# Three of four z blocks turned by VectorE, the second output product over two column blocks at a time, and the identity first on SP's queue

## What is computed

```python
def conformer_mixer(hn, w_in, b_in, w_dw, b_dw, ln_g, ln_b, w_out, b_out):
    proj = hn @ w_in
    ab = proj[..., :2 * CONV_WIDTH] + b_in
    z = proj[..., 2 * CONV_WIDTH:]
    a, g = jnp.split(ab, 2, axis=-1)
    u = a * jax.nn.sigmoid(g)
    u = lax.conv_general_dilated(
        u, w_dw[:, None, :].astype(u.dtype), window_strides=(1,),
        padding=((CONV_K - 1, 0),), dimension_numbers=('NWC', 'WIO', 'NWC'),
        feature_group_count=CONV_WIDTH) + b_dw
    u = jax.nn.silu(layer_norm(u, ln_g, ln_b))
    return (u * jax.nn.silu(z)) @ w_out + b_out
...
        x = x + rms_norm(y, post_norm_g[i])
```

## Time and profile before

| | |
|---|---|
| median of 3 runs | 850.21 us (847.71 to 851.01) |
| the profiled execution | 850.66 us, its span 848.9 us |
| TensorE busy | 837.6 us, 99% of the span |
| VectorE, ScalarE, GpSimd busy | 684.5, 428.2, 336.4 us |
| DMA | 159.49 MB, mean 188 GB/s |

### The profile page before, as it was taken

How to read it: one execution, slowest core, us unless ns; L and a number is a source line. 1 busy time by engine, 2 the same in 40 slices (tenths; PEclk the granted TensorE clock), 3 DMA queues, 4 the chain that set the end, 5 groups by cost and what they waited for, 6 DMA issues and landing times.

```text
span 848.9 us, 12103 instructions
## 1 busy us (share of the span) xinstructions
PE 837.6 (99%) x3873; PEld 695.4 (82%) x3873; DVE 684.5 (81%) x1179; ACT 428.2 (50%) x592; POOL 336.4 (40%) x169
## 2 busy tenths in 40 slices
PE   8999999999999999999999999999999999999996
PEld 6888888888888888888888788888888888888884
DVE  4688799988999799968656629999999999566555
ACT  5744544455444645454445674545444554574441
POOL 0243004500441014400000299888888878772000
PEclk9999999999999999999999999999999999999999
DMA  9956655656467545746655366555655546556522
GB/s 320 293 164 199 195 151 171 194 182 198 150 189 213 188 150 170 225 148 219 215 188 193 129 199 199 187 174 184 198 179 172 194 156 198 191 212 236 197 98 99
DMA packets 97509, 159.49 MB, mean 188 GB/s; under 512 B 3300, under 2 KB 38468, under 8 KB 97092
## 3 DMA queue, kind: packets, MB, share of 16 engines
q1 hardware_dynamic: 97284, 158.97, 58.5%
q10 hardware_dynamic: 192, 0.08, 0.0%
HBM read 156.94 MB, written 2.10 MB: 187 GB/s over the span
## 4 chain that ended last, share of the span: by engine, by line
PE 97%; issue 1%; DMA 1%; DVE 0%; ACT 0%; DVEq 0%; POOLq 0%; POOL 0%; ACTq 0%
PE acc L420 29%; PE acc L422 29%; PE acc L421 29%; PE X L430 2%; PE acc L405 1%; PE acc L407 1%; PE acc L406 1%; PE acc L501 1%; PE acc L486 1%; DMA ident<-in_identity 1%; PE X L560 0%; PE X L545 0%; PE X L544 0%; PE X L561 0%; PE X L559 0%
## 5 line engine op out<-in xcount | busy, mean ns | idle before, releaser
L773 ACT ACTIVATE w_hi<-raw 128x1024 fp32r<-128x1024 f32 x282 | 298.8, 1061 | 354.4 <-PE acc L422 354.0
L420 PE MATMUL acc<-w_hi,xT_hi 128*128 128x512 f32 x864 | 339.0, 392 | 0.1
L422 PE MATMUL acc<-w_hi,xT_lo 128*128 128x512 f32 x864 | 336.5, 389 | 0.0
L421 PE MATMUL acc<-w_lo,xT_hi 128*128 128x512 f32 x864 | 336.2, 389 | 0.0
L1059 DVE TENSOR_TENSOR w_lo<-raw,w_hi 128x1024 fp32r<-128x1024 f32 x182 | 245.7, 1366 | 78.9 <-ACT w_hi L773 76.6
L1518 POOL TENSOR_TENSOR w_lo<-raw,w_hi 128x1024 fp32r<-128x1024 f32 x100 | 243.1, 2438 | 48.9 <-ACT w_hi L773 48.7
L422 PEld LDWEIGHTS acc<-w_hi,xT_lo 128*128 128x128 f32 x864 | 162.2, 188 | 34.0
L420 PEld LDWEIGHTS acc<-w_hi,xT_hi 128*128 128x128 f32 x864 | 162.3, 188 | 33.1 <-DVE xT_lo L1078 0.3
L421 PEld LDWEIGHTS acc<-w_lo,xT_hi 128*128 128x128 f32 x864 | 162.3, 188 | 32.9
L1343 DVE SCALAR_TENSOR_TENSOR X<-u_pad,taps,X 128x256 f32<-128x256 f32 x464 | 182.5, 480 | 0.0
L1481 POOL TENSOR_TENSOR small<-small 128x1 f32<-128x1 f32 (+1 forms) x7 | 4.3, 618 | 232.9 <-DVE small L1289 124.2
(11 more groups left out here) (151 smaller groups left out, 755.0 us busy)
## 6 DMA issues: line engine op xcount, KB each, us to landing
raw<-in_w_in SPq DMA_DIRECT2D x78, 1024.0 KB, 5.3
raw<-in_w_in SPq DMA_DIRECT2D x66, 512.0 KB, 4.4
raw<-in_w_out SPq DMA_DIRECT2D x32, 1024.0 KB, 5.0
gpost<-in_post_g SPq DMA_DIRECT2D x2, 1024.0 KB, 5.0
xrow<-in_x SPq DMA_DIRECT2D x4, 256.0 KB, 5.5
raw<-in_w_in SPq DMA_DIRECT2D x4, 256.0 KB, 4.9
xrow<-in_x SPq DMA_DIRECT2D x2, 512.0 KB, 10.0
bout<-in_b_out SPq DMA_DIRECT2D x1, 1024.0 KB, 7.3
```

What stands on the lines that cost most here:

```text
L420: nc.tensor.matmul(a, hi[:, k, rows], w_hi[:, slot, i], start=(k == 0), stop=False)
L421: nc.tensor.matmul(a, hi[:, k, rows], w_lo[:, slot, i], start=False, stop=False)
L422: last = nc.tensor.matmul(a, lo[:, k, rows], w_hi[:, slot, i], start=False, stop=(k == KT - 1))
L773: nc.scalar.activation(w_hi[:, slot], raw[:, u % LOADS, 2 * half:2 * half + 2], ACT.Copy).then_inc(hi_ready[slot], 1)
```

## The change

- `ident` is loaded first on SP's queue instead of second on ScalarE's. Four of the seven `keep_clock` matmuls stand ahead of the wait, three between the transpose of the norm gains and that of x.
- z blocks 0 to 2 are no longer turned by TensorE. VectorE turns them in SBUF with `turn` (four instructions of 32 x 32 block transposes a step, four steps a block) into a new buffer `zT`, which lies where `c_row` did. `gate` reads blocks 0 to 2 there in one instruction each; block 3 is turned by TensorE as before (`last_gate_T`), now without a wait for gate 2.
- The output product goes through column blocks 0 and 1 together, four k tiles of each in turn (`OUT1_ORDER`), then blocks 2 and 3 as before. The loads, the waits for `vT_lo` (now ahead of slices 0, 4, 8, 12), the reading of blocks 0 and 1 (`OUT1_LAST`, behind the splits of slices 17 and 19) and the sums of squares follow.
- ScalarE rounds the gated blocks behind slices 0, 3, 5 and 9 (`FINAL_AT`) instead of 0, 2, 4 and 6, and writes z rows of block 3 ahead of the second.
- GpSimd splits slices 0 to 9 (`OUT1_POOL`) instead of 0 to 7.
- `gpost1` and `bout` are loaded into the space of `xT_lo`, once the last z slice is multiplied, instead of over `z_row1` once the last z transposes are done.

```diff
-GATE_AT = (26, 28, 30)
+OUT1_ORDER = tuple([(n, k + i) for k in (0, 2, 4, 6) for n in (0, 1) for i in (0, 1)]
+                   + [(n, i) for n in (2, 3) for i in range(SLICES)])
+OUT1_LAST = (13, 15, 23, 31)
+OUT1_POOL = 10
+FINAL_AT = (0, 3, 5, 9)
...
-        gpost1 = at("gpost1", B + 16 * KB, [P, D])
-        bout = at("bout", B + 24 * KB, [P, D])
+        zT = at("zT", B, [P, KT - G, SEQ])
+        gpost1 = at("gpost1", A + 16 * KB, [P, D])
+        bout = at("bout", A + 24 * KB, [P, D])
...
+            sp.dma_start(ident[:], identity).then_inc(ident_in, 16)
             x_load(0, 0)
...
             for j in range(16):
-                load(S_OUT1, 0, 32, j, w_out1[0], (j // 4) * NCOL)
+                n, part = OUT1_ORDER[2 * j]
+                load(S_OUT1, 0, 32, j, w_out1[0], n * NCOL, part // 2)
                 if j == 5:
-                    sp.wait_ge(zT_done, NG)
+                    sp.wait_ge(w_used[RING - 1], rounds(S_OUT1, 0, 0, -1))
...
-            keep_clock(7)
+            keep_clock(4)
             pe.wait_ge(ident_in, 16)
             pe.wait_ge(pre_in, 16)
             nc.tensor.transpose(X[3][:, 0:NPRE], pre_rows[:], ident[0:NPRE, 0:NPRE]).then_inc(vec_T, 1)
+            keep_clock(3)
...
-                if s in GATE_AT:
-                    gate_T(GATE_AT.index(s))
...
             for s in range(4 * SLICES):
-                if s % SLICES == 0:
-                    acc_free(32 + s // SLICES)
-                if s < SLICES and s % 2 == 0:
-                    pe.wait_ge(vlo_ready, s // 2 + 1)
+                n, part = OUT1_ORDER[s]
+                if part == 0:
+                    acc_free(32 + n)
+                if n == 0 and part % 2 == 0:
+                    pe.wait_ge(vlo_ready, part // 2 + 1)
                 if s < 4 * SLICES - RING:
-                    slice_products(S_OUT1, 0, 0, s, vT_hi, vT_lo)
+                    slice_products(S_OUT1, 0, 0, s, vT_hi, vT_lo, (n, part))
                 if s == 1:
-                    gate_T(NG - 1)
+                    last_gate_T()
...
                 high(S_OUT1, 0, 0, s)
-                if s in (0, 2, 4, 6):
-                    final_high(s // 2)
                 if s == 3:
                     block_rows(S_Z, 0, 0, 31, z_row1[:, :, 3 * NCOL:4 * NCOL], rms[2], ACT.Silu)
+                if s in FINAL_AT:
+                    final_high(FINAL_AT.index(s))
...
+            def turn_gate(n, steps):
+                if steps[0] == 0:
+                    dve.wait_ge(rows_out, 28 + n + 1)
+                for a in steps:
+                    turn(zT[:, G * n:G * (n + 1)], z_row1[:, :, n * NCOL:(n + 1) * NCOL], a, z_turned)
...
                 dve.wait_ge(silu_ready, n + 1)
-                dve.wait_ge(zT_done, n + 1)
-                for b in range(2):
-                    part = cT[:, 4 * n + 2 * b:4 * n + 2 * b + 2]
-                    last = nc.vector.tensor_tensor(part, part, X[2 + b][:].rearrange("p (t r) -> p t r", t=2), ALU.mult)
+                if n < NG - 1:
+                    dve.wait_ge(z_turned, 4 * (n + 1))
+                    c = cT[:, 4 * n:4 * n + 4]
+                    last = nc.vector.tensor_tensor(c, c, zT[:, 4 * n:4 * n + 4], ALU.mult)
+                else:
+                    dve.wait_ge(zT_done, 1)
...
```

More of the change, by code:

```diff
@@ L238, in build @@
         zT_done = sem("zT_done")
+        z_turned = sem("z_turned")
         silu_ready = sem("silu_ready")
@@ L701, in statistics_wide, with last_gate_T @@
                 last.then_inc(stat_ready, 1)
[L703 to L707, removed]
+            def last_gate_T():
+                pe.wait_ge(rows_out, 28 + NG)
                 for b in range(2):
-                    last = pair_T(z_row1, X[2 + b], 4 * n + 2 * b)
+                    last = pair_T(z_row1, X[2 + b], G * (NG - 1) + 2 * b)
                 last.then_inc(zT_done, 1)
@@ L812, in _ @@
             act.dma_start(pre_rows[:], pre_g.rearrange("l (t c) -> (l t) c", c=P)).then_inc(pre_in, 16)
-            act.dma_start(ident[:], identity).then_inc(ident_in, 16)
             act.wait_ge(vec_T, 1)
@@ L1359, in _, with row_stats @@
                         conv_tap(h * 2 + c, c, k, h * per_pair + 2 * k - 1 + c)
-            for n in range(NG):
+            def row_stats(n):
                 for m in range(MT):
@@ L1370, in _ @@
                     nc.vector.bn_stats(bn[:, m, n], rows).then_inc(bn_ready, 1)
+            def turn_gate(n, steps):
[3 more added lines that the diff above has]
+                    turn(zT[:, G * n:G * (n + 1)], z_row1[:, :, n * NCOL:(n + 1) * NCOL], a, z_turned)
+            for n in range(NG - 1):
+                row_stats(n)
+            dve.wait_ge(bn_ready, MT * (NG - 1))
+            turn_gate(0, (0, 1))
+            row_stats(NG - 1)
             dve.wait_ge(bn_ready, MT * NG)
@@ L1388, in gate @@
                 dve.wait_ge(silu_ready, n + 1)
-                dve.wait_ge(zT_done, n + 1)
-                for b in range(2):
-                    part = cT[:, 4 * n + 2 * b:4 * n + 2 * b + 2]
-                    last = nc.vector.tensor_tensor(part, part, X[2 + b][:].rearrange("p (t r) -> p t r", t=2), ALU.mult)
+                if n < NG - 1:
[4 more added lines that the diff above has]
+                    dve.wait_ge(zT_done, 1)
+                    for b in range(2):
+                        c = cT[:, 4 * n + 2 * b:4 * n + 2 * b + 2]
+                        last = nc.vector.tensor_tensor(c, c, X[2 + b][:].rearrange("p (t r) -> p t r", t=2), ALU.mult)
                 last.then_inc(t_ready, 1)
@@ L1399, in final_low @@
                                         vT_hi[:, 4 * n:4 * n + 4].bitcast(f32), ALU.subtract).then_inc(vlo_ready, 1)
+            turn_gate(0, (2, 3))
+            turn_gate(1, (0,))
             normalise(0)
             normalise(1)
+            turn_gate(1, (1,))
             gate(0)
             normalise(2)
+            final_low(0)
+            turn_gate(1, (2, 3))
             gate(1)
-            final_low(0)
             normalise(3)
+            final_low(1)
+            turn_gate(2, range(4))
             gate(2)
-            final_low(1)
             gate(3)
@@ L1432, in out1_gained @@
                 nc.vector.tensor_tensor(yg1[:, m, c], y1[:, m, c], gpost1[:, c], ALU.mult).then_inc(yg_ready, 1)
-            for s in range(SLICES, 4 * SLICES):
+            for s in range(OUT1_POOL, 4 * SLICES):
                 low(S_OUT1, 0, 0, s)
-                if s % SLICES == 3:
+                if s in (17, 19, 27):
+                    n = (17, 19, 27).index(s)
                     for m in range(MT):
-                        out1_biased(s // SLICES - 1, m)
+                        out1_biased(n, m)
                     for m in range(MT):
-                        out1_gained(s // SLICES - 1, m)
+                        out1_gained(n, m)
             mean_but_last(30, 4)
@@ L1534, in _ @@
                 low(S_Z, 0, 0, s)
-            for s in range(SLICES):
+            for s in range(OUT1_POOL):
                 low(S_OUT1, 0, 0, s)
```

6 lines of the change are left out of this document (3 added, 3 removed).

## The result

| | before | after |
|---|---|---|
| median (lowest to highest) | 849.19 us (847.52 to 851.01), 8 runs | 852.57 us (851.26 to 853.45), 8 runs |
| the profiled execution | 850.66 us, span 848.9 | 851.74 us, span 849.9 |
| TensorE busy | 837.6 us, 99% | 835.0 us, 98% |
| VectorE, ScalarE, GpSimd busy | 684.5, 428.2, 336.4 us | 704.3, 428.1, 340.4 us |
| DMA | 159.49 MB | 159.50 MB |

The ratio is 1.0041, interval 1.0031 to 1.0051: slower by 3.5 us, 2.6 to 4.3. The forecast of 852.2 us is 0.4 us from the median. The difference was forecast less well: +2.0 on the 850.21 of the three runs then shown, where eight runs of before have a median of 849.19. The profiled execution of before lies 1.5 us above that median.

A forecast was written before the change was run, and what follows sets the result against it. TensorE's chain, 97% of the span, was taken as the bound, so any new TensorE wait counts in full. From 850.66: -2.6 transposes, -1.2 start, +5.8 VectorE's new work give 852.65, or 852.2 us against the median; range 846.0 to 855.2.

The forecast's parts named there:

- The removed transposes: TensorE, z blocks: three of four transpose groups go, 0.88 us each, -2.6 us.
- The start: Earlier identity brings the first product to about 6.8 us instead of 7.40 and an earlier clock rise; together -1.2 us.
- if that distance stays: Start: TensorE reaches 2.4 GHz 5.8 us after its work begins, as before, so at about 9.7 us.
- The walk through VectorE: Output product: turns and gates meeting GpSimd's splits delay ScalarE; TensorE waits 1.7 us at slice 4, 3.1 at slice 6.
- Slices 8 and 9: Output product: GpSimd's last splits, formerly VectorE's, alternate with VectorE's own; +1.0 us.
- Rival (d): The 3.1 us pause ahead of slice 6 drops TensorE to 1.2 GHz, costing 2.9: 855.1 us; chance 0.07.
- (b): One or two VectorE meetings with GpSimd fall VectorE's way: waits of 1.7 to 3.6, 848.1 to 850.0 us; chance 0.26.
- (c): VectorE's chain keeps up, collisions being milder, and TensorE doesn't wait: 846.4 us; chance 0.16.
- (e): VectorE's turns collide with GpSimd as well: 21 us of waits, 867 us; chance 0.05.
- the wait at slice 16: Output product: sign that block 0's bank isn't back in time, its 5.4 us cover failing; up to 1 us.
- matmuls 0.43 us apart after the pause: TensorE behind the pause ahead of slice 6: sign against the forecast, for the drop to 1.2 GHz.

The follow-up runs named there:

- the start alone: Kernel before with only the change's start: identity first on SP's queue, idle matmuls split four and three; 848.70 us, ratio 0.9992.
- run with a PSUM operand: Changed kernel with gates 0 to 2 reading a PSUM operand in place of `zT`, silu(z) left out of three blocks; 848.81 us, ratio 0.9998.
- filled waits: Changed kernel with five idle matmuls ahead of slice 4 of the output product and ten ahead of slice 6; 852.02 us, ratio 1.0028.
- the start undone: Changed kernel with identity second on ScalarE's queue again and seven idle matmuls at once; 852.99 us, ratio 1.0042.
- the kernel block by block: Changed kernel with the output product, its roundings and GpSimd's eight splits as before, turns and gates kept; 856.81 us, ratio 1.0090.

## Why the forecast was right

**The removed transposes: right.** -2.6 forecast, -2.58 between the two traces at slice 2 of the output product (-2.70 at its first matmul).

**The start: mis-sized.** -1.2 forecast; 0.5 and 0.4 in the medians of the two runs that isolate it; neither can be told from nothing, and the interval of the first still holds 1.2. Two steps of it failed. The identity landed 2.0 us after its issue, not the 3.2 of a load four times as large, so the first product began at 6.2 to 6.3 and not at 6.8. And "if that distance stays" was no basis: the rise came by 11.8 in before, by 9.5 with the start alone and ahead of 6.3 in after. I had taken a random moment of one execution for a property of the kernel. The reference was shifted in the same way: 850.66, the profiled execution, is 1.5 us above the eight-run median, where I said 0.45.

**The walk through VectorE: right, step by step.** The walk's times have no start in them, so 2.99 us are taken off.

| | walk | less 2.99 | trace |
|---|---|---|---|
| gate 0 done | 744.1 | 741.1 | 741.12 |
| low part 0 done | 749.8 | 746.8 | 746.84 |
| gate 1 done | 755.6 | 752.6 | 752.55 |
| gate 2 done | 767.5 | 764.5 | 764.55 |
| slice 4 split | 763.5 | 760.5 | first matmul 760.59 |
| slice 6 split | 772.1 | 769.1 | first matmul 769.17 |

Waits of 1.7 and 3.1 were forecast, 1.75 and 3.02 came. The rule behind it, that a VectorE operation with both inputs in SBUF ends 1.1 us after GpSimd's split, held in all three meetings, and the closest one, low part 0, went as I had chosen. The run with a PSUM operand shows the mechanism itself. The Trainium skill ("SBUF — State Buffer", § Who interferes with whom) has it as one rule: two SBUF inputs contend with a GpSimd instruction that reads SBUF, one input outside the two-port modes doesn't. The traces agree, on both sides: 3.05 against 1.22 us for the gate, and 1.8 for every turn.

**Slices 8 and 9: +1.0 forecast, not seen as a wait.** The late splits were there, but in after the slow stretch stood over them. Where the clock stayed up they cost what was forecast: from the start of slice 6 to that of slice 10 pass 11.89 us with filled waits and 11.90 with gates from PSUM, where four slices in full stream take 10.88. That is 1.0.

**The clock: a rival's event inside the forecast.** Rival (d) had 0.07 and came true in its mechanism: after the pause ahead of slice 6 the clock fell to 1.2 GHz. It cost 1.6 us and not 2.9, because the clock was back 4.0 us after the restart, 3.4 of them at the lower level, where I had taken 5.8 from the start. Of the 1.6 only 0.75 comes back with filled waits (103.00 against 102.25); the rest hid the late slices. The chance was too low. My sentence "no row of a pause at full clock exists here" was an argument for not knowing, and I used it as one against. By the skill's rule that I quoted there ("TensorE: Matmul & The Clock Gate", § What's actually happening) the clock would fall if the pause was long enough; here it fell after the 2.9 us and not after the 1.6 us ahead of slice 4.

**Sum in medians.** -2.6 (transposes) - 0.5 (start) + 4.8 (waits) + 1.6 (clock) = +3.3; measured +3.4. Forecast, without the base: -2.6 - 1.2 + 5.8 = +2.0. So the absolute time was right within 0.4 us partly because errors cancelled: the base was 1.0 too high (850.21 for 849.19), the start 0.7 too good, the clock's 1.6 left out, and the 1.0 of slices 8 and 9 counted, which the slow stretch covered.

**The other rivals.** (b) would have needed one meeting to go VectorE's way, none did. (c) is excluded by the two waits. (e) is excluded: 48 turns between 425 and 444 ns, also beside GpSimd. The falsifiers did their work: the wait at slice 16 did not come, and "matmuls 0.43 us apart after the pause" did.

**What the forecast didn't see** is how cheap the remedy was. The walk put ScalarE's rounding of block 2 ahead of slice 6 as a fact of the change; but the new order of the output product needs that block at slice 8 only. Two numbers in ScalarE's order and the place of one silu turn +3.4 us into -4.0 in medians. By the stages the part that is not the start's is 2.4 under before: 2.70 for the transposes, less 0.26.

## What to carry to other kernels

Where work moves to an engine off the critical path, walk that engine's program with its times and ask who stands in line behind its results on the next engine: here 21 us of added work cost nothing once two roundings and a silu no longer stood ahead of weight slices. The loss needed both, late results and that order: fewer turns or gates that don't wait each took 4.2 of its 6.8 us away too. In a kernel like this one, price every VectorE operation with two SBUF inputs beside a GpSimd instruction as waiting for its end, and give it one PSUM operand where that is to be had. After a wait of TensorE look at the spacing of the matmuls behind it too, since no list of waits shows a lower clock; and take what a start is worth from medians of many runs, not from two profiles.

## What was not expected of the hardware

- After an idle stretch of 2.86 us TensorE's clock fell to 1.2 GHz, 0.6 us after it had started again (769.74; with the start undone at once, in the kernel block by block 1.6 us after the pause of 2.61, and 0.6 us after the second of two pauses of 2.41 and 1.21), and came back 3.4 us after that. After 1.58 us of idleness it did not fall. Idle matmuls in the pause prevented it.
- The same start code reached 2.4 GHz by 9.5 us in one execution and ahead of 6.3 in another. In six traces with that start and the same TensorE work up to there the output product begins between 746.65 and 748.84. Executions of one kernel spread by up to 3.5 us; how much of that is the rise was not measured.
- A load of 64 KB at the head of SP's queue landed in 2.0 us, the same load as the second on ScalarE's queue in 4.5.
